# Seven-product weight sums by accumulating transfers from GpSimd, with the products rearranged so that every weight sum is an addition

## The chip, the cores and the metric

One core of one Trainium2 chip runs the whole program. The metric is the device time of one execution in microseconds (us), the median of several runs; smaller is better.

## What is computed

The reference is two layers of a decoder trunk for one sequence of 256 tokens with 1024 channels. A layer is a SwiGLU block (`ffn1`), a token mixer (a diagonal state-space group beside a gated group), and a second SwiGLU block (`ffn2`), each behind an RMSNorm and added to the residual stream:

```
for l in range(2):
    x = x + 0.5 * swiglu(rmsnorm(x, norm_ffn1[l]), ffn1_w_in[l], ffn1_w_out[l])
    x = x + mixer(rmsnorm(x, norm_mix[l]))
    x = x + 0.5 * swiglu(rmsnorm(x, norm_ffn2[l]), ffn2_w_in[l], ffn2_w_out[l])
swiglu(h, w_in, w_out): g, u = split(h @ w_in); return (silu(g) * u) @ w_out     # 1024 -> 2 x 2816 -> 1024
```

All data are float32. The change lies in the last product of `ffn2`, `(silu(g) * u) @ ffn2_w_out`, with 2816 rows of weights.

## The kernel before

**Precision and the weight stream.** Each matmul operand is split into a high part (`w_hi`, rounded to the fp32r type by ScalarE) and a remainder (`w_lo`, by VectorE), and a product is three matmuls: high by high, high by low, low by high. SyncE loads the weights in slots of 1 MB (`raw`, three of them); a slot is two "halves" of 128x1024 weights, and the stream has 152 halves for each layer. ScalarE makes `w_hi` of a half (L1016), VectorE its `w_lo` (L1324). Both have a ring of four halves, so ScalarE starts the split of half n when TensorE is done with half n-4. SyncE loads into a slot when VectorE has split what lay there.

**The order of the work.** Every engine has one written-out order. In `ffn2` ScalarE and VectorE run a loop over h (halves 0 to 43 are the input weights, 44 to 65 the output weights): gates (`gate`, L1070) and hidden tiles at given h, then the split of half h, then at given h the work on the weight sums.

**Seven products.** For six pairs of 128-row tiles of `ffn2_w_out` (SEVEN, L72) the 2x2 blocks are multiplied with seven products in place of eight (Winograd's form). With B11, B12 the two column halves of the first row tile and B21, B22 of the second, it needs four sums of weights T1 to T4 (and four of hidden blocks, S1 to S4). Such a pair is called sum m here, m = 0 to 5 within a layer. Its steps:

- SyncE loads both row tiles into an area of four 128x512 quarters, in two transfers of 512 KB (`load_sums`, L375 to L390), at h = 26, 28, 36, 38, 52, 54 of its own, earlier order (LOAD_AT, L76). Areas 0 and 1 (`sums_b`) serve sums 0 to 3, two further ones (`area`) sums 4 and 5.
- VectorE forms T1 to T4 in place with four subtractions (`sums_make`, L1327 to L1340), at h = 25, 29, 36, 41, 53, 56 (SUMS_AT, L77). T2 needs T1, and T4 needs T2.
- ScalarE splits the 128x2048 area into `s_hi` (`sums_split`, L986 to L994) and VectorE into `s_lo` (L1342 to L1348), at h = 28, 31, 55, 57, 59, 61 (SPLIT_AT, L78). `s_hi` and `s_lo` have two buffers. On ScalarE the step stands behind the split of half h and ahead of the split of half h+1, in one queue.
- TensorE does the seven products (`seven_rows`, L729): three with the plain weights, then four that wait for `s_lo`.

GpSimd prepares the mixer's tables, does the mixer's small operations (`mix`, L1840 to L1876) and the reciprocal square roots of the norms (`norm`, L1667). It issues no transfers. In `ffn2` it waits for the next norm.

Of the kernel before, what the change touches and what calls it, by code (L numbers as in the profile page):

```python
# [11 lines left out]
ALU = mybir.AluOpType  # L12
# [7 lines left out]
UB = FF // 256  # L20
# [53 lines left out]

AREA = (0, 1, 0, 1, 2, 3)
LOAD_AT = (26, 28, 36, 38, 4 * UB + 8, 4 * UB + 10)  # L76
SUMS_AT = (25, 29, 36, 41, 4 * UB + 9, 4 * UB + 12)  # L77
SPLIT_AT = (28, 31, 4 * UB + 11, 4 * UB + 13, 4 * UB + 15, 4 * UB + 17)  # L78
FOLD_AT = 4 * UB + 2 * SEVEN[-1] + 5

S3, S1, S2, S4 = range(4)
T3, T1, T2, T4 = range(4)

B11, B22, B21 = range(3)

# [28 lines left out]
def norm_no(l, i):  # L114
    return 3 * l + i
# [23 lines left out]
def build(nc, a, out):  # L139
    stack = ExitStack()  # L140
    with stack:
# [169 lines left out]
        def hidden_bank(l, j, b):  # L311

            c0, _, t0, t1_ = ROLES[l, stage_of(2 * j)]
            if b == UB - 1:
                return bank[2 * c0]
            return bank[2 * (t1_ if b in (2, 3, 6, 7) else t0) + b % 2]
# [15 lines left out]
        def _(sp):  # L332
# [42 lines left out]
            def load_sums(l, h):  # L375

                for i in range(N7):
                    if LOAD_AT[i] == h:
                        m = l * N7 + i
                        if i == 0:  # L380
                            sp.wait_ge(half_done, half(l, UP2) + 1)
                        if i in (2, 3):
                            sp.wait_ge(slo_done, m - 1)
                        if i > 3:
                            sp.wait_ge(half_done, half(l, DN2))
                        k = 2 * SEVEN[i]
                        src = a["ffn2_w_out"][l, k * P:(k + 2) * P, :].rearrange("(t p) m -> p t m", p=P)
                        dst = areas[AREA[i]].rearrange("p (t c m) -> p t c m", t=2, c=2)
                        for c in range(2):
                            sp.dma_start(dst[:, :, 1 - c, :], src[:, :, c * 512:c * 512 + 512]).then_inc(s_full[AREA[i]], 16)  # L390

            def load_ffn(l, j):
                w_in, w_out = (a["ffn1_w_in"], a["ffn2_w_in"])[j], (a["ffn1_w_out"], a["ffn2_w_out"])[j]
# [589 lines left out]
        def _(act):  # L983
            A = nc.scalar.activation

            def sums_split(l, h):  # L986

                for i in range(N7):
                    if SPLIT_AT[i] == h:
                        m = l * N7 + i  # L990
                        act.wait_ge(sb_done, 4 * m + 4)
                        if m > 1:
                            act.wait_ge(seven_done, m - 1)
                        A(s_hi[:, m % 2, :], areas[AREA[i]], ACT.Copy).then_inc(shi_done, 1)  # L994
# [87 lines left out]
            def hidden_hi(l, j, b):  # L1082
                act.wait_ge(hT_done, UB * (2 * l + j) + b + 1)
                if j and b in SEVEN:
                    m = l * N7 + SEVEN.index(b)
                    act.wait_ge(sa_done, 3 * m)
                    A(a21[:, 0, :], hidden_bank(l, j, b)[:, P:2 * P], ACT.Copy)
                    A(a21[:, 1, :], hidden_bank(l, j, b)[:, P:2 * P], ACT.Copy, scale=-1.0).then_inc(a21_done, 1)
                A(h_hi[:, 2 * b:2 * b + 2, :].rearrange("p k c -> p (k c)"), hidden_bank(l, j, b)[:, :],
                  ACT.Copy).then_inc(hhi_done, 1)  # L1090

# [214 lines left out]
        def _(dve):  # L1306
# [17 lines left out]
                TT(w_lo[:, n % RING, :], raw[:, s, (n % 2) * 1024:(n % 2) * 1024 + 1024],  # L1324
                   w_hi[:, n % RING, :].bitcast(F32), ALU.subtract).then_inc(lo_done, 1)

            def sums_make(l, h):  # L1327

                for i in range(N7):
                    if SUMS_AT[i] == h:  # L1330
                        m = l * N7 + i
                        q = areas[AREA[i]].rearrange("p (i m) -> p i m", i=4)
                        dve.wait_ge(*sums_full(m))
                        TT(q[:, T1, :], q[:, 0, :], q[:, T1, :], ALU.subtract).then_inc(sb_done, 1)
                        dve.wait_ge(sb_done, 4 * m + 1)
                        TT(q[:, T3, :], q[:, 0, :], q[:, 2, :], ALU.subtract).then_inc(sb_done, 1)
                        dve.wait_ge(sb_done, 4 * m + 2)
                        TT(q[:, T2, :], q[:, 2, :], q[:, T1, :], ALU.subtract).then_inc(sb_done, 1)
                        dve.wait_ge(sb_done, 4 * m + 3)
                        TT(q[:, T4, :], q[:, 3, :], q[:, T2, :], ALU.subtract).then_inc(sb_done, 1)  # L1340

            def sums_split(l, h):  # L1342

                for i in range(N7):
# [86 lines left out]
            def hidden_lo(l, j, b):  # L1431
                if j and b in SEVEN:
                    m = l * N7 + SEVEN.index(b)
                    tiles = hidden_bank(l, j, b)[:, :].rearrange("p (i m) -> p i m", i=4)
                    dve.wait_ge(a21_done, m + 1)
                    if m > 0:
                        dve.wait_ge(salo_done, m)
                    dve.wait_ge(hhi_done, UB * (2 * l + j) + b + 1)
                    TT(sums_a[:, 0:2, :], tiles[:, 0:4:3, :], a21[:, :, :], ALU.subtract).then_inc(sa_done, 1)
                    dve.wait_ge(sa_done, 3 * m + 1)  # L1440
                    TT(sums_a[:, S2, :], sums_a[:, S1, :], tiles[:, 0, :], ALU.subtract).then_inc(sa_done, 1)
                    dve.wait_ge(sa_done, 3 * m + 2)
                    TT(sums_a[:, S4, :], tiles[:, 2, :], sums_a[:, S2, :], ALU.subtract).then_inc(sa_done, 1)
                dve.wait_ge(hhi_done, UB * (2 * l + j) + b + 1)
                TT(h_lo[:, 2 * b:2 * b + 2, :].rearrange("p k c -> p (k c)"), hidden_bank(l, j, b)[:, :],  # L1445
                   h_hi[:, 2 * b:2 * b + 2, :].rearrange("p k c -> p (k c)").bitcast(F32),
                   ALU.subtract).then_inc(hlo_done, 1)
# [7 lines left out]
            def fold(l, j):  # L1455


                c0, c1, t0, t1_ = ROLES[l, "ffn2"]
                p5, p6, p7 = bank[2 * c0 + 1], bank[2 * t0], bank[2 * t0 + 1]
                p1, u2, u3 = (sums_b[:, 0, i * 512:i * 512 + 512] for i in range(3))  # L1460
                xb = [[x[:, t, c * 512:c * 512 + 512] for c in range(2)] for t in range(2)]
                n = 8 * l
                dve.wait_ge(p1_done, l + 1)
                STT(u2, p6[:, :], 0.5, p1, ALU.mult, ALU.add).then_inc(fold_done, 1)
                STT(xb[0][1], p5[:, :], 0.5, xb[0][1], ALU.mult, ALU.add).then_inc(fold_done, 1)
                STT(xb[1][1], p5[:, :], 0.5, xb[1][1], ALU.mult, ALU.add).then_inc(fold_done, 1)
                TT(xb[0][0], xb[0][0], p1, ALU.add).then_inc(fold_done, 1)
                dve.wait_ge(fold_done, n + 4)
                STT(u3, p7[:, :], -0.5, u2, ALU.mult, ALU.add).then_inc(fold_done, 1)
                TT(xb[0][1], xb[0][1], u2, ALU.add).then_inc(fold_done, 1)  # L1470
                dve.wait_ge(fold_done, n + 5)
                TT(xb[1][0], xb[1][0], u3, ALU.add).then_inc(fold_done, 1)
                TT(xb[1][1], xb[1][1], u3, ALU.add).then_inc(fold_done, 1)

            def ffn(l, j):
                f = 2 * l + j
                if f == 0:
                    first_in()
                elif j == 0:
                    norm_in(l, 0, UPS[j], ACC_FFN2, (0.5, 0.5), DN2 + FT - 1)  # L1480
                else:
                    norm_in(l, 2, UPS[j], ACC_SSM, (ors[:, 2:3], ors[:, 3:4]), OUT + KT - 1)
                for h in range(4 if f else 5, 4 * UB + FT + 1):
                    if h in GATES_AT[f]:
                        hidden(l, j, GATES_AT[f][h])
                    split(l, UPS[j] + h)
                    if j:
                        sums_split(l, h)
                        sums_make(l, h)
                    if j and h - 1 in HIDDEN_AT and HIDDEN_AT.index(h - 1) in SEVEN:  # L1490
                        sums_lo(l, HIDDEN_AT.index(h - 1))
                    if h in HIDDEN_AT:
                        hidden_lo(l, j, HIDDEN_AT.index(h))
                    if j and h == FOLD_AT:
                        fold(l, j)
# [146 lines left out]
        def _(pool):  # L1642
# [197 lines left out]
            def mix(l):  # L1840
# [34 lines left out]
                inv_sqrt(ors[:, 2:4], oms[:, 2:4], ors_done)  # L1875
                norm(norm_no(l, 2))  # L1876

            link(nc.gpsimd.memset(ident[:, :], 0.0))
            link(nc.gpsimd.affine_select(out=ident[:, :], in_=ident[:, :], compare_op=ALU.not_equal, fill=1.0,
                                         base=0, pattern=[[-1, P]], channel_multiplier=1))  # L1880
# [14 lines left out]
            prep_rest(0)  # L1895
            restart()
            mix(0)
            norm(norm_no(1, 0))
            pool.wait_ge(half_done, half(1, 0))
            clear_blocks()  # L1900
# [1 line left out]
            prep_rest(1)  # L1902
            restart()
            mix(1)
            pool.wait_ge(ms_done, 3 * DEPTH + 1)
            inv_sqrt(rstd_c[:, 0:1], ms_c[:, 0:1], rstd_done)
            pool.wait_ge(x_done, residuals(DEPTH - 1, ACC_FFN2) + 3)
# [22 lines left out]
```

## Time and profile before

| | us |
|---|---|
| median of 3 runs (908.05 to 908.76) | 908.31 |
| the profiled execution, time | 907.8 |
| the profiled execution, span on the core | 906.1 |

The profile is of one execution. Its span leaves out 1.7 us that lie around it. The views used below are the page (busy time by engine, DMA issues), the waits (who waited for whom, longest first), the timeline (instructions in order of time), the windows (busy time and DMA share in given stretches) and the instructions of one tile. PE is TensorE, PEld its weight loads, ACT ScalarE, DVE VectorE, POOL GpSimd, SP SyncE; "SPq" is what SyncE's queue issued. TensorE's granted clock is 0.999 over the span. Layer 0's `ffn2` runs from about 270 to 453 us, layer 1's from about 717 to 900 us.

### The profile page before, as it was taken

How to read it: one execution, taken by the hardware profiler on the slowest of the kernel's cores; microseconds unless marked ns; L12 is line 12 of the kernel's file. 1: busy time of each engine (PE TensorE's matmuls, PEld its weight loads, DVE VectorE, ACT ScalarE, POOL GpSimd, SP SyncE). 2: the span in 40 equal slices, each digit the busy share in tenths (PEclk: the TensorE clock that was granted, in tenths of full speed). 3: DMA queues.
4: the chain of work that ended last, by engine and by line, in shares of the span. 5: the costliest groups of instructions: out<-in, count | busy, mean ns of one | idle time of the engine just before them, and what ended most of it. 6: DMA issues, size and time to landing. Idle time of an engine off the chain costs nothing.

```text
span 906.1 us, 12882 instructions
## 1 busy us (share of the span) xinstructions
PE 897.4 (99%) x4935; PEld 743.1 (82%) x4935; DVE 620.3 (68%) x729; ACT 507.4 (56%) x741; POOL 371.8 (41%) x574
## 2 busy tenths in 40 slices
PE   9999999999999999999999999999999999999997
PEld 7888888888878888887888888888888888888886
DVE  5555665458976578868965656653888855789597
ACT  6544454458766456646464445445677654656474
POOL 3488999894510000000055889988734100000000
PEclk9999999999999999999999999999999999999999
DMA  9786555544256677684559665555344476785751
GB/s 281 196 271 188 186 184 180 175 160 142 94 194 200 196 251 230 229 283 159 186 175 246 186 188 186 186 186 186 120 160 143 139 221 196 263 270 188 267 175 46
DMA packets 138381, 174.60 MB, mean 193 GB/s; under 512 B 18760, under 2 KB 110032, under 8 KB 138320
## 3 DMA queue, kind: packets, MB, share of 16 engines
q1 hardware_dynamic: 138032, 173.24, 59.7%
q8 instruction: 39, 0.64, 0.3%
q10 hardware_dynamic: 288, 0.53, 0.2%
q14 instruction: 22, 0.18, 0.1%
HBM read 172.70 MB, written 1.05 MB: 192 GB/s over the span
## 4 chain that ended last, share of the span: by engine, by line
PE 95%; DVE 3%; issue 1%; DMA 1%; ACT 1%; SPq 0%; ACTq 0%; DVEq 0%
PE bank L501 29%; PE bank L503 29%; PE bank L502 29%; PE bank L606 2%; DVE w_lo L1319 1%; PE bank L511 1%; PE bank L833 1%; DVE s_lo L1348 1%; DMA raw<-in_ffn_w_in 1%; PE bank L861 0%; PE bank L851 0%; PE bank L874 0%; PE bank L716 0%; ACT w_hi L1007 0%; PE bank L937 0%
## 5 line engine op out<-in xcount | busy, mean ns | idle before, releaser
L1324 DVE TENSOR_TENSOR w_lo<-raw,w_hi 128x1024 fp32r<-128x1024 f32 x278 | 351.0, 1271 | 214.4 <-ACT w_hi L1016 214.2
L1016 ACT ACTIVATE w_hi<-raw 128x1024 fp32r<-128x1024 f32 x278 | 292.7, 1061 | 242.0 <-PE bank L503 223.2
L501 PE MATMUL bank<-w_hi,x_hi 128*128 128x512 f32 x856 | 336.5, 393 | 0.0
L503 PE MATMUL bank<-w_hi,x_lo 128*128 128x512 f32 x856 | 333.5, 390 | 0.0
L502 PE MATMUL bank<-w_lo,x_hi 128*128 128x512 f32 x856 | 333.2, 389 | 0.0
L501 PEld LDWEIGHTS bank<-w_hi,x_hi 128*128 128x128 f32 x856 | 160.7, 188 | 35.2 <-issue 2.5
L503 PEld LDWEIGHTS bank<-w_hi,x_lo 128*128 128x128 f32 x856 | 160.7, 188 | 33.7
L502 PEld LDWEIGHTS bank<-w_lo,x_hi 128*128 128x128 f32 x856 | 160.8, 188 | 32.3
L1664 POOL TENSOR_TENSOR rstd_c<-ms_c,neg_half 128x2 f32<-128x2 f32 (+1 forms) x7 | 7.7, 1106 | 394.9 <-DVE ms_c L1367 394.9
L501 PE MATMUL bank<-w_hi,h_hi 128*128 128x512 f32 (+1 forms) x283 | 111.0, 392 | 0.0
L503 PE MATMUL bank<-w_hi,h_lo 128*128 128x512 f32 (+1 forms) x283 | 109.7, 387 | 0.0
L502 PE MATMUL bank<-w_lo,h_hi 128*128 128x512 f32 (+1 forms) x283 | 109.6, 387 | 0.0
L1079 ACT ACTIVATE sil<-bank,rstd_c 128x256 f32<-128x256 f32 x88 | 36.8, 470 | 53.2 <-PE bank L503 53.1
L501 PEld LDWEIGHTS bank<-w_hi,h_hi 128*128 128x128 f32 x283 | 53.1, 188 | 11.4 <-DVE h_lo L1445 0.6
L503 PEld LDWEIGHTS bank<-w_hi,h_lo 128*128 128x128 f32 x283 | 53.1, 188 | 11.0
L502 PEld LDWEIGHTS bank<-w_lo,h_hi 128*128 128x128 f32 x283 | 53.2, 188 | 10.4
L1655 POOL TENSOR_TENSOR sc<-sc 128x16 f32<-128x16 f32 (+1 forms) x154 | 55.2, 358 | 12.3
L1428 DVE SCALAR_TENSOR_TENSOR hid<-bank,rstd_c,sil 128x256 f32<-128x256 f32 x88 | 38.5, 479 | 24.4 <-ACT sil L1079 24.4
L1655 POOL TENSOR_TENSOR pt<-sc,bp 128x256 f32<-128x256 f32 x56 | 52.6, 940 | 4.4
L1658 POOL TENSOR_SCALAR sc<-sc 128x16 f32<-128x16 f32 (+1 forms) x90 | 38.7, 430 | 7.7
L1655 POOL TENSOR_TENSOR bp<-pt 128x256 f32<-128x256 f32 x32 | 36.3, 1133 | 2.5
L1319 DVE TENSOR_TENSOR w_lo<-raw,w_hi 128x1536 fp32r<-128x1536 f32 x12 | 21.0, 1753 | 12.9 <-ACT w_hi L1007 12.9
(231 smaller groups left out, 886.9 us busy)
## 6 DMA issues: line engine op xcount, KB each, us to landing
raw<-in_ffn_w_in SPq DMA_DIRECT2D x172, 512.0 KB
raw<-in_ffn_w_out SPq DMA_DIRECT2D x32, 1024.0 KB
raw<-in_mix_w_in SPq DMA_DIRECT2D x12, 1024.0 KB
raw<-in_mix_w_out SPq DMA_DIRECT2D x8, 1024.0 KB
sums_b<-in_ffn_w_out SPq DMA_DIRECT2D x16, 512.0 KB, 6.9
raw<-in_ffn_w_out SPq DMA_DIRECT2D x12, 512.0 KB
area<-in_ffn_w_out SPq DMA_DIRECT2D x8, 512.0 KB, 6.4
raw<-in_ffn_w_out SPq DMA_DIRECT2D x12, 256.0 KB
```

Of the source, the lines that this page charges most:

```text
L501: mm(o, hi_a, hi_b, start=first, stop=False)
L502: mm(o, hi_a, lo_b, start=False, stop=False)
L503: return mm(o, lo_a, hi_b, start=False, stop=last)
L511: ins = nc.tensor.transpose(turned(pair, j)[:, h * P:h * P + P], x[:, h, k * P:k * P + P], ident[:, :])
L606: ins = nc.tensor.transpose(hidden_bank(l, j, b)[:, c:c + P], hid[:, b % 4, h, ft * P:ft * P + P], ident[:, :])
L1016: A(w_hi[:, n % RING, :], raw[:, s, (n % 2) * 1024:(n % 2) * 1024 + 1024], ACT.Copy).then_inc(hi_done, 1)
L1079: A(sil[:, b % 2, t, :], bank[2 * pair + t][:, 0:256], ACT.Silu, scale=rstd_c[:, t:t + 1]).then_inc(sil_done, 1)
L1319: TT(w_lo[:, n % RING:n % RING + 2, :].rearrange("p s m -> p (s m)")[:, 0:1536], raw[:, s, 0:1536], w_hi[:, n % RING:n % RING + 2, :].rear ...
L1324: TT(w_lo[:, n % RING, :], raw[:, s, (n % 2) * 1024:(n % 2) * 1024 + 1024], w_hi[:, n % RING, :].bitcast(F32), ALU.subtract).then_inc(lo_d ...
L1428: STT(hid[:, b % 4, t, :], bank[2 * pair + t][:, 256:512], rstd_c[:, t:t + 1], sil[:, b % 2, t, :], ALU.mult, ALU.mult).then_inc(hid_done, 1)
L1655: link(nc.gpsimd.tensor_tensor(o, x0, x1, op))
L1658: link(nc.gpsimd.tensor_scalar(o, x0, s1, s2, op0, op1))
```

## The change

The four sums of a pair are formed without VectorE. SyncE loads B12 into two quarters (a source that is repeated), and B21, B22 into the other two. GpSimd then issues four transfers that add to their destination in SBUF: T1 = B12 + B11 and T3 = B12 + B22 from HBM; when both have landed, T2 = B22 + T1, and when that has landed, T4 = B21 + T2, both from SBUF to SBUF. It waits for the last of each sum before the next sum. All six sums of a layer stand in GpSimd's order between `mix` and the next layer's first norm. ScalarE's split waits for the semaphore that these transfers raise. The signs move to the hidden sums (`a21`, `sums_a`), where two copies of ScalarE become one, and to the fold at the stage's end.

```diff
-SUMS_AT = (25, 29, 36, 41, 4 * UB + 9, 4 * UB + 12)
...
-T3, T1, T2, T4 = range(4)
+T1, T3, T4, T2 = range(4)
...
# load_sums (SyncE)
-                        dst = areas[AREA[i]].rearrange("p (t c m) -> p t c m", t=2, c=2)
-                        for c in range(2):
-                            sp.dma_start(dst[:, :, 1 - c, :], src[:, :, c * 512:c * 512 + 512]).then_inc(s_full[AREA[i]], 16)
+                        dst = areas[AREA[i]].rearrange("p (t m) -> p t m", t=2)
+                        b12 = src[:, 0, 512:1024].unsqueeze(1).broadcast_to([P, 2, 512])
+                        sp.dma_start(dst[:, 0, :].rearrange("p (c m) -> p c m", c=2), b12).then_inc(s_full[AREA[i]], 16)
+                        sp.dma_start(dst[:, 1, :], src[:, 1, :]).then_inc(s_full[AREA[i]], 16)
...
# sums_split (ScalarE)
-                        act.wait_ge(sb_done, 4 * m + 4)
+                        act.wait_ge(sb_done, 64 * m + 64)
...
# hidden_hi (ScalarE)
-                    A(a21[:, 0, :], hidden_bank(l, j, b)[:, P:2 * P], ACT.Copy)
-                    A(a21[:, 1, :], hidden_bank(l, j, b)[:, P:2 * P], ACT.Copy, scale=-1.0).then_inc(a21_done, 1)
+                    A(a21[:, :, :], hidden_bank(l, j, b)[:, :].rearrange("p (i m) -> p i m", i=4)[:, 1:4:2, :],
+                      ACT.Copy).then_inc(a21_done, 1)
...
# sums_make leaves VectorE (four subtractions for each sum)
-                        TT(q[:, T1, :], q[:, 0, :], q[:, T1, :], ALU.subtract).then_inc(sb_done, 1)
...
# hidden_lo (VectorE)
-                    TT(sums_a[:, 0:2, :], tiles[:, 0:4:3, :], a21[:, :, :], ALU.subtract).then_inc(sa_done, 1)
+                    TT(sums_a[:, 0:2, :], tiles[:, 0:2, :], a21[:, :, :], ALU.subtract).then_inc(sa_done, 1)
...
-                    TT(sums_a[:, S4, :], tiles[:, 2, :], sums_a[:, S2, :], ALU.subtract).then_inc(sa_done, 1)
+                    TT(sums_a[:, S4, :], tiles[:, 2, :], sums_a[:, S2, :], ALU.add).then_inc(sa_done, 1)
...
# fold (VectorE): the same eight operations, three of them with another sign
...
# new on GpSimd, called as sums_make(0) behind mix(0) and sums_make(1) behind mix(1)
+            def sums_make(l):
+                for i in range(N7):
+                    m = l * N7 + i
+                    k = 2 * SEVEN[i]
+                    b1, b2 = (a["ffn2_w_out"][l, (k + t) * P:(k + t + 1) * P, :] for t in range(2))
+                    q = areas[AREA[i]].rearrange("p (i m) -> p i m", i=4)
+                    pool.wait_ge(*sums_full(m))
+                    pool.dma_start(q[:, T1, :], b1[:, 0:512], accum_op=ALU.add).then_inc(sb_done, 16)
+                    pool.dma_start(q[:, T3, :], b2[:, 512:1024], accum_op=ALU.add).then_inc(sb_done, 16)
+                    pool.wait_ge(sb_done, 64 * m + 32)
+                    pool.dma_start(q[:, T2, :], q[:, T1, :], accum_op=ALU.add).then_inc(sb_done, 16)
+                    pool.wait_ge(sb_done, 64 * m + 48)
+                    pool.dma_start(q[:, T4, :], q[:, T2, :], accum_op=ALU.add).then_inc(sb_done, 16)
+                    pool.wait_ge(sb_done, 64 * m + 64)
```

## Rows read from the trace of the kernel before

**Rows 1.** The page, busy time of each engine, its share and instructions.

```profile
PE 897.4 (99%) x4935; PEld 743.1 (82%) x4935; DVE 620.3 (68%) x729; ACT 507.4 (56%) x741; POOL 371.8 (41%) x574
```

**Rows 2.** The waits, whole run: who waited for whom; total us, times, longest us.

```profile
POOL rstd_c L1664 <- DVE ms_c L1367: 394.9, 7, 182.5
ACT w_hi L1016 <- PE bank L503: 223.2, 153, 3.0
...
PEld bank L501 <- DVE s_lo L1348: 1.5, 2, 0.7
```

**Rows 3.** Timeline, 424 to 432 us: start, duration, engine, line, operation, [idle before].

```profile
425.23 0.68 DVE L1334 TENSOR_TENSOR area<-area 128x512 f32<-128x512 f32 x1
...
428.01 2.28 DVE L1348 TENSOR_TENSOR s_lo<-sums_b,s_hi 128x2048 fp32r<-128x2048 f32 x1
...
429.64 0.39 PE L503 MATMUL bank<-w_hi,h_lo 128*128 128x512 f32 x1
...
430.34 0.19 PEld L501 LDWEIGHTS bank<-s_hi,hs_hi 128*128 128x128 f32 x1 [0.74 <-DVE s_lo L1348]
```

**Rows 4.** Instructions of the tile sums_b: duration in ns, minimum/median/maximum, first and last start.

```profile
L1334 DVE TENSOR_TENSOR sums_b<-sums_b x8: 684/684/685, 336.5 to 831.3; 128x512 f32<-128x512 f32 x8
...
L994 ACT ACTIVATE s_hi<-sums_b x8: 1900/1918/1930, 343.4 to 869.6; 128x2048 fp32r<-128x2048 f32 x8
```

**Rows 5.** Timeline of SyncE's queue, 318 to 370 and 764 to 830 us.

```profile
324.89 1.02 SPq L390 DMA_DIRECT2D sums_b<-in_ffn_w_out  x2
...
332.82 1.02 SPq L390 DMA_DIRECT2D sums_b<-in_ffn_w_out  x2
336.63 18.93 SPq L345 DMA_DIRECT2D raw<-in_ffn_w_in  x8
...
771.76 1.02 SPq L390 DMA_DIRECT2D sums_b<-in_ffn_w_out  x2
```

**Rows 6.** DMA issues between 325.2 and 326.0 us: KB each, median us to landing.

```profile
sums_b<-in_ffn_w_out SPq DMA_DIRECT2D x2, 512.0 KB, 6.3
```

**Rows 7.** Timeline of ScalarE, 322 to 376 and 785 to 810 us.

```profile
343.42 1.90 ACT L994 ACTIVATE s_hi<-sums_b 128x2048 fp32r<-128x2048 f32 x1
...
350.55 0.84 ACT L1079 ACTIVATE sil<-bank,rstd_c 128x256 f32<-128x256 f32 x2 [1.60 <-PE bank L503]
...
352.23 1.92 ACT L994 ACTIVATE s_hi<-sums_b 128x2048 fp32r<-128x2048 f32 x1
...
361.43 0.84 ACT L1079 ACTIVATE sil<-bank,rstd_c 128x256 f32<-128x256 f32 x2 [1.60 <-PE bank L503]
...
807.73 0.84 ACT L1079 ACTIVATE sil<-bank,rstd_c 128x256 f32<-128x256 f32 x2 [1.60 <-PE bank L503]
```

**Rows 8.** Timeline of VectorE, 322 to 352 us.

```profile
345.35 2.29 DVE L1348 TENSOR_TENSOR s_lo<-sums_b,s_hi 128x2048 fp32r<-128x2048 f32 x1 [0.58 <-ACT s_hi L994]
347.56 1.22 DVE L1324 TENSOR_TENSOR w_lo<-raw,w_hi 128x1024 fp32r<-128x1024 f32 x1
```

**Rows 9.** Windows, all engines: busy us by engine (count), PEclk, DMA share, GB/s.

```profile
332.00:340.00 8.00, 8.00 (x37) 6.63 (x36) 7.60 (x13) 4.42 (x8) 0.00 (x0) 1.00 0.85 291
340.00:348.00 8.00, 8.00 (x37) 6.64 (x36) 6.91 (x7) 5.38 (x7) 0.00 (x0) 1.00 0.73 235
348.00:356.00 8.00, 8.00 (x37) 6.62 (x36) 7.90 (x10) 5.50 (x7) 0.00 (x0) 1.00 0.45 137
```

**Rows 10.** DMA issues of the run: count, KB each, median us from issue to landing.

```profile
raw<-in_ffn_w_in SPq DMA_DIRECT2D x8, 256.0 KB, 4.7
...
out<-x SPq DMA_DIRECT2D x6, 128.0 KB, 2.1
```

**Rows 11.** The tile sums_b: landing times of its sixteen loads.

```profile
DMA to landing us min/median/max: 6.0/6.9/8.6
```

**Rows 12.** The page, costliest groups: the only GpSimd group on the norms.

```profile
L1664 POOL TENSOR_TENSOR rstd_c<-ms_c,neg_half 128x2 f32<-128x2 f32 (+1 forms) x7 | 7.7, 1106 | 394.9 <-DVE ms_c L1367 394.9
```

**Rows 13.** Timeline of TensorE, 439 to 441 us.

```profile
440.00 0.39 PE L501 MATMUL bank<-s_hi,hs_hi_last 128*128 128x512 f32 x1
```

More of the change, by code:

```diff
@@ L1325, in split @@
                    w_hi[:, n % RING, :].bitcast(F32), ALU.subtract).then_inc(lo_done, 1)
[L1327 to L1333, printed above, removed]
-                        TT(q[:, T1, :], q[:, 0, :], q[:, T1, :], ALU.subtract).then_inc(sb_done, 1)
[L1335 to L1340, printed above, removed]
             def sums_split(l, h):
@@ L1468, in fold @@
                 dve.wait_ge(fold_done, n + 4)
-                STT(u3, p7[:, :], -0.5, u2, ALU.mult, ALU.add).then_inc(fold_done, 1)
-                TT(xb[0][1], xb[0][1], u2, ALU.add).then_inc(fold_done, 1)
+                STT(u3, p7[:, :], 0.5, u2, ALU.mult, ALU.add).then_inc(fold_done, 1)
+                TT(xb[0][1], xb[0][1], u2, ALU.subtract).then_inc(fold_done, 1)
                 dve.wait_ge(fold_done, n + 5)
                 TT(xb[1][0], xb[1][0], u3, ALU.add).then_inc(fold_done, 1)
-                TT(xb[1][1], xb[1][1], u3, ALU.add).then_inc(fold_done, 1)
+                TT(xb[1][1], xb[1][1], u3, ALU.subtract).then_inc(fold_done, 1)
             def ffn(l, j):
@@ L1488, in ffn @@
                         sums_split(l, h)
-                        sums_make(l, h)
                     if j and h - 1 in HIDDEN_AT and HIDDEN_AT.index(h - 1) in SEVEN:
@@ L1897, in _ @@
             mix(0)
+            sums_make(0)
             norm(norm_no(1, 0))
@@ L1904, in _ @@
             mix(1)
+            sums_make(1)
             pool.wait_ge(ms_done, 3 * DEPTH + 1)
```

## The prediction, made before the changed kernel was run

> **What bounds the kernel now.** I read the busy times first: TensorE works 897.4 of the 906.1 us of the span, 99% [rows 1]. So the kernel can only become faster where TensorE stands still, and slower wherever something new makes it stand still. The waits come next. ScalarE waits for TensorE 153 times in the weight splits alone, 223.2 us in all, while the waits of TensorE's weight loads for VectorE's `s_lo` are two, one in each layer [rows 2]. The engines that prepare weights are ahead of TensorE and are paced by its ring of four halves. VectorE's 620.3 us are therefore mostly cover, not path.
>
> The one place where the sums on VectorE hurt is seen in the timeline. From 425.23 us VectorE makes the last pair's four sums, and only at 428.01 does it start an `s_lo` whose `s_hi` was ready before; TensorE's last matmul starts at 429.64, the next weight load at 430.34 [rows 3]. At the pace of 0.23 us between matmuls (2.72 us for twelve, below) it should have come at 429.87, so about 0.5 us are lost, and 0.1 us more as the first matmul starts cold. That is 0.6 us, in each layer.
>
> **What the change removes.** Twelve sums of four subtractions leave VectorE: 48 x 0.69 us = 33 us [rows 4], which is 5% of its busy time. All but the sums of rows 3 lie in time that VectorE has. With them gone, the `s_lo` of rows 3 starts some 2.7 us earlier, and both stalls go: **-1.2 us** for the two layers. That is the whole gain that I can find. Twelve copies of ScalarE, the other signs in the fold and in the hidden sums, and the new quarters cost or give nothing: the copies lie beside ScalarE's 223 us of waiting [rows 2], the rest are the same operations on the same shapes. SyncE still issues two transfers of 512 KB for a sum.
>
> **What it adds.** GpSimd gets 48 transfers of 256 KB and waits for them. Behind them in its queue stands only the next layer's norm; GpSimd waits 394.9 us for VectorE's means anyway [rows 2], so the wait costs there nothing. What waits for the transfers is ScalarE: the split of the area stands in its queue ahead of the next weight split. So the question is when the chain of a sum ends: landing, then the pair T1 and T3, then T2, then T4, three steps in series, and the second sum's chain only behind the first's.
>
> *When they may end.* Sum 0 is split at 343.42, sum 1 at 352.23 [rows 7], but later would do. The gates wait for halves 27 and 31; they start at 350.55 and 361.43 [rows 7], so a half takes 10.88/4 = 2.72 us, half 29 begins at 353.3 and half 32 at 361.4. Behind a late sum 1 stand ScalarE's `s_hi` (1.92 us [rows 4]), VectorE's `s_lo` (2.29) and `w_lo` of half 32 (1.22) [rows 8], and some 0.2 us of signals: 5.6 us. So sum 1 must be ready at 361.4 - 5.6 = **355.8**, and sum 0 in the same way at 347.7. In layer 1 the way from the first load's issue (771.76) to the same gate (807.73) is 36.0 us against 36.5 in layer 0 [rows 5, 7]: 0.6 us less room.
>
> *When they can begin.* Sum 0's second load is issued at about 325.4 [rows 5] and lands 6.3 us later [rows 6], at 331.7. Sum 1's loads, issued from 332.82, land by 340, before sum 0's chain is through. So both chains together may take 355.8 - 331.7 = **24.1 us**.
>
> *What a chain takes.* No row shows a transfer from GpSimd or one that adds. From below: a quiet 128 KB store takes 2.1 us from issue to landing [rows 10]. The queue moves 291 GB/s at a share of 0.85 [rows 9], 342 GB/s when full, so its 128 KB are 0.38 us of that and 256 KB are 0.77. A step is then at least 2.5 us, the pair 3.3, a chain 8.3, two chains 16.6: no stall. From above: every step like the slowest load of 8.6 us [rows 11], 25.8 us for a chain. Between them I build a step from three terms. The fixed part is 2.1 - 0.38 - 0.5 (SyncE's own issue, half of 1.02 [rows 5]) = 1.2 us. The issue by GpSimd I take as its small operation, 1.1 us [rows 12], as its instructions cost more than SyncE's. The data take 0.77 us once, or 1.54 if the destination's reading counts like a second transfer; where SyncE's queue is full they take twice as long, since the two share the same 16 engines. It is nearly full from 332 to 343 (share 0.85, then 0.73, with the weights issued at 336.63 [rows 5]), and far less from 348 (0.45 [rows 9]).
>
> - Data once: sum 0 is pair 5.4 + T2 3.8 + T4 3.1 = 12.3 us; sum 1, in the quiet part, 3.8 + 3.1 + 3.1 = 10.0. Both 22.3: in time.
> - Data twice: 8.5 + 5.4 + 3.8 = 17.7 and 5.4 + 3.8 + 3.8 = 13.0. Both 30.7: sum 1 is ready at 362.4, 6.6 us late, and 7.2 us late in layer 1.
>
> I take the middle, 26.5 us, which makes a busy step 4.6 us, close to the 4.7 us of SyncE's 256 KB loads at the kernel's busy start [rows 10]. Sum 1 is then ready at 358.2: 2.4 us late, 3.0 us in layer 1. TensorE stands still for that time, as its ring of halves has run dry; nothing later gives it back, as TensorE is busy for 99% of the span [rows 1]. The other four sums have room: at 13.3 us a chain the sixth would end at 331.7 + 80 = 412, and TensorE wants it at 440.00 [rows 13], less 4.4 us for its splits.
>
> Weights delayed by the sharing cost nothing: those issued at 336.63 are split from about 347.9 on, and the extra 1 MB (2 if counted twice) of sum 0 is 3 to 6 us of the queue's time; were the cover gone, it would be 1 to 2 us a layer.
>
> **The sum.** -1.2 + 2.4 + 3.0 = +4.2 us on the profiled execution's 907.8 us, 912.0. That execution is 0.5 us below the median of 908.3, so I predict **912.5 us**.
>
> **The rivals.**
> *In time.* Both chains fit into 24.1 us, ScalarE never waits, and only the gain is left: 908.3 - 1.2 = 907.1 us, not slower. For it speaks the bound from below, and the sum with data counted once; against it the full queue at the very time of sum 0 [rows 9]. It decides at 12 us a chain. The Trainium skill (DMA: Bandwidth & Descriptors, Anatomy of one DMA) gives a transfer issued by GpSimd 2.0 us plus its bytes at 436 GB/s, all told: by that, as an estimate, 2.6 us a step, 0.6 more for the pair, 8.4 us a chain and 907.1 us. The page's fit is for plain copies; no run so far shows one here.
> *Six in series.* If adding is much slower than copying, the six chains of a layer follow each other past the stage's end: the sixth must be ready at 440.0 - 4.4 = 435.6, so from (435.6 - 331.7)/6 = 17.3 us a chain it rules. At 20 us it ends 16.1 us late in each layer, +31 us, 939 us; at the upper bound of 25.8 us, 50.9 late, +101, 1009 us. Against it: it needs steps like the slowest loads, also in the quiet parts.
> *VectorE's relief pays more.* 33 us are taken off VectorE, but the waits of TensorE's weight loads for `s_lo` add up to 1.5 us [rows 2]; over 1.8 us could only come from something that no wait shows.
>
> **How the numbers follow.** What a measurement of this kernel can tell from no change is about 0.2%, 1.8 us. The stall of sum 1 has 0.50, with its own range from 909 to 925 us (data twice gives 921.5, and a slower issue lies above). In time has 0.35, six in series 0.11, more relief 0.04. Faster by over 0.2% is the last alone, 0.04. Within 0.2% is the rival in time and the edge of the stall where it eats the gain, 0.36. Slower is the rest, 0.60. The range goes from 906.8, just under the rival in time, to 936, which leaves out most of six in series.
>
> **What the changed profile would show.** The wait of ScalarE's L994 for GpSimd's transfers, long for sum 1 of each layer, near 352 and 798 us of the old time, and behind it waits of TensorE for `w_lo` of a few us: the forecast. No such wait, and landing times of 2 to 3.5 us: the rival in time. L994 waiting at the sixth sum: six in series. The stall behind rows 3 should be gone in any case. I am wrong if TensorE stands still elsewhere, above all for weights from SyncE, or if GpSimd's issue or the adding takes times outside my bounds.

## The result, and the profile after

The changed kernel takes 972.4 us (median of five runs, 968.3 to 974.3) against 908.1 us: a ratio of 1.0694, 95% interval 1.0677 to 1.0711, or 64 us more. The prediction was slower, 912.5 us, with a range up to 936. The direction was right, the size was not: it lies in the span that the rival *six in series* was given, 939 to 1009 us.

The page of the profile after (span 972.5 us), busy times, answers to [rows 1]:

```profile
span 972.5 us, 12882 instructions
...
PE 912.2 (94%) x4935; PEld 752.4 (77%) x4935; DVE 589.8 (61%) x681; ACT 505.4 (52%) x729; POOL 415.1 (43%) x622
```

TensorE has the same 4935 matmuls. It stands still for 972.5 - 912.2 = 60.3 us, against 8.7 us before: +51.6. And it is busy 14.8 us longer. Together that is the 66.4 us by which the spans differ. VectorE lost 30.5 us of work, and nothing came of it.

The waits of the profile after (total us, times, longest us) tell for what:

```profile
ACT s_hi L994 <- DMA sums_b<-sums_b: 50.5, 4, 14.3
...
PE bank L501 <- DVE w_lo L1324: 32.1, 4, 9.7
...
ACT s_hi L994 <- DMA area<-area: 28.0, 3, 13.5
...
PE bank L501 <- DVE s_lo L1333: 19.6, 2, 9.9
```

GpSimd waits for each landing before it issues the next step. ScalarE's `s_hi` waits for the last landing, and behind it stands the weight split. TensorE then waits for `w_lo`, four times in all, two in each layer; and for the `s_lo` of the sixth sum, once in each. 32.1 + 19.6 = 51.7 us are the whole +51.6.

The timeline of GpSimd in layer 0 shows the chains of sums 0 and 1, L1870 being T1, L1873 T2 and L1875 T4, with L1871 (T3) directly behind each L1870 (start, duration, then in brackets the wait before):

```profile
334.03 1.10 POOL L1870 DMA_DIRECT2D sums_b<-in_ffn_w_out  x1 [54.58 <-DMA sums_b<-in_ffn_w_out]
...
345.65 0.88 POOL L1873 DMA_DIRECT2D sums_b<-sums_b  x1 [9.59 <-DMA sums_b<-in_ffn_w_out]
352.41 0.90 POOL L1875 DMA_DIRECT2D sums_b<-sums_b  x1 [5.89 <-DMA sums_b<-sums_b]
355.99 0.89 POOL L1870 DMA_DIRECT2D sums_b<-in_ffn_w_out  x1 [2.67 <-DMA sums_b<-sums_b]
...
362.44 0.87 POOL L1873 DMA_DIRECT2D sums_b<-sums_b  x1 [4.66 <-DMA sums_b<-in_ffn_w_out]
368.08 0.90 POOL L1875 DMA_DIRECT2D sums_b<-sums_b  x1 [4.76 <-DMA sums_b<-sums_b]
375.52 0.89 POOL L1870 DMA_DIRECT2D sums_b<-in_ffn_w_out  x1 [6.54 <-DMA sums_b<-sums_b]
```

Sum 0 takes 21.7 us from its first issue to ScalarE's start (355.73 below), sum 1 a further 19.5. ScalarE's timeline, the three splits that waited:

```profile
355.73 1.91 ACT L994 ACTIVATE s_hi<-sums_b 128x2048 fp32r<-128x2048 f32 x1 [11.23 <-DMA sums_b<-sums_b]
...
375.26 1.91 ACT L994 ACTIVATE s_hi<-sums_b 128x2048 fp32r<-128x2048 f32 x1 [14.06 <-DMA sums_b<-sums_b]
...
466.69 1.91 ACT L994 ACTIVATE s_hi<-area 128x2048 fp32r<-128x2048 f32 x1 [13.55 <-DMA area<-area]
```

They answer to 343.42 and 352.23 in [rows 7] and to the sixth sum, for which the prediction worked out 435.6 from [rows 13].

The early stops also hold back what comes later. SyncE issues the load of sum 4, the fifth of the layer, 21.5 us later than before the change, and GpSimd waits for it before it can begin that chain (first line from the kernel before, the other two from the changed kernel):

```profile
395.86 0.88 SPq L390 DMA_DIRECT2D area<-in_ffn_w_out  x2
...
417.36 0.37 SPq L389 DMA_DIRECT2D area<-in_ffn_w_out  x1
...
425.38 0.88 POOL L1870 DMA_DIRECT2D area<-in_ffn_w_out  x1 [10.93 <-DMA area<-in_ffn_w_out]
```

The windows of layer 0 (busy us of PE, PEld, DVE, ACT, POOL with counts, granted clock, DMA share, GB/s) show what a stop does to TensorE's clock:

```profile
335.00:345.00 10.00, 10.00 (x46) 8.27 (x45) 6.92 (x11) 5.49 (x7) 1.06 (x2) 1.00 1.04 296
...
355.00:365.00 10.00, 3.85 (x11) 3.06 (x12) 6.48 (x6) 5.47 (x6) 2.67 (x3) 0.66 0.61 133
365.00:375.00 10.00, 6.04 (x27) 4.67 (x25) 0.00 (x0) 0.00 (x0) 0.90 (x1) 0.97 1.01 291
375.00:385.00 10.00, 4.22 (x11) 3.35 (x12) 7.62 (x7) 6.42 (x7) 2.60 (x3) 0.51 0.49 90
```

In the stretches where TensorE starts again after a stop the mean granted clock is 0.66 and 0.51; the timeline has the matmuls at 363 us 0.43 us apart, from 364.3 on 0.23. So TensorE restarts at the lower level, 1.2 GHz, and the timeline shows the same slower pace behind all six stops, which are 6.6 to 9.9 us long. Against 0.23 us a matmul the matmuls behind the stops lose 13.9 us, 1.5 to 2.9 us a stop, which is nearly all of the 14.8 us of longer busy time. GpSimd's queue and its transfers in the DMA view (packets, MB and share of the 16 engines' span; KB each, median us from issue to landing):

```profile
q0 software_dynamic: 6912, 12.59, 7.6%
...
sums_b<-in_ffn_w_out POOLq DMA_DIRECT2D x16, 256.0 KB, 5.9
sums_b<-sums_b POOLq DMA_DIRECT2D x16, 256.0 KB, 6.3
...
area<-in_ffn_w_out POOLq DMA_DIRECT2D x8, 256.0 KB, 7.0
area<-area POOLq DMA_DIRECT2D x8, 256.0 KB, 4.3
```

### The profile page after: what moved, and what is told of

It is laid out like the page before. It is cut to its first block, busy times and chain, and to the rows that moved or that the text cites. A ratio compares the mean times of both kernels' runs of the same rounds, so it can differ in the third digit from the quotient of the medians.

```text
span 972.5 us, 12882 instructions
## 1 busy us (share of the span) xinstructions
PE 912.2 (94%) x4935; PEld 752.4 (77%) x4935; DVE 589.8 (61%) x681; ACT 505.4 (52%) x729; POOL 415.1 (43%) x622
## 3 DMA queue, kind: packets, MB, share of 16 engines
q0 software_dynamic: 6912, 12.59, 7.6%
## 4 chain that ended last, share of the span: by engine, by line
PE 75%; DMA 16%; issue 4%; DVE 2%; ACT 1%; SPq 1%; POOL 1%; POOLq 0%; ACTq 0%
PE bank L501 23%; PE bank L502 23%; PE bank L503 23%; DMA sums_b<-in_ffn_w_out 5%; DMA area<-in_ffn_w_out 4%; DMA sums_b<-sums_b 3%; DMA area<-area 3%; PE bank L606 1%; DVE s_lo L1333 1%; PE bank L511 1%; PE bank L833 1%; ACT s_hi L994 1%; DMA x<-in_x 1%; DVE w_lo L1324 0%; PE bank L861 0%
## 5 line engine op out<-in xcount | busy, mean ns | idle before, releaser
L501 PE MATMUL bank<-w_hi,x_hi 128*128 128x512 f32 x856 | 340.9, 398 | 32.1 <-DVE w_lo L1324 32.1
L502 PE MATMUL bank<-w_lo,x_hi 128*128 128x512 f32 x856 | 336.6, 393 | 0.0
L501 PEld LDWEIGHTS bank<-w_hi,x_hi 128*128 128x128 f32 x856 | 163.0, 190 | 69.8 <-issue 21.9
L503 PEld LDWEIGHTS bank<-w_hi,x_lo 128*128 128x128 f32 x856 | 162.7, 190 | 34.7
L502 PEld LDWEIGHTS bank<-w_lo,x_hi 128*128 128x128 f32 x856 | 163.1, 191 | 32.9
L1870 POOL DMA_DIRECT2D sums_b<-in_ffn_w_out x8 | 7.4, 920 | 140.8 <-DMA sums_b<-in_ffn_w_out 109.7
L1639 POOL TENSOR_TENSOR sc<-sc 128x16 f32<-128x16 f32 (+1 forms) x154 | 59.6, 387 | 12.3
L502 PEld LDWEIGHTS bank<-w_lo,h_hi 128*128 128x128 f32 x283 | 53.3, 188 | 10.4
L1333 DVE TENSOR_TENSOR s_lo<-sums_b,s_hi 128x2048 fp32r<-128x2048 f32 x8 | 18.3, 2293 | 54.0 <-ACT s_hi L994 54.0
L994 ACT ACTIVATE s_hi<-sums_b 128x2048 fp32r<-128x2048 f32 x8 | 15.3, 1914 | 55.3 <-DMA sums_b<-sums_b 50.5
```

What stands on the lines that cost most here:

```text
L501: mm(o, hi_a, hi_b, start=first, stop=False)
L502: mm(o, hi_a, lo_b, start=False, stop=False)
L503: return mm(o, lo_a, hi_b, start=False, stop=last)
L1333: TT(s_lo[:, m % 2, :], areas[AREA[i]], s_hi[:, m % 2, :].bitcast(F32), ALU.subtract).then_inc(slo_done, 1)
L1639: link(nc.gpsimd.tensor_tensor(o, x0, x1, op))
```

## The experiments

The comparison for each is the kernel before on the same chip. "Changed" means that the edit is made in the changed kernel.

**The form alone (e1).** The kernel before with the four subtractions of `sums_make` as additions and the signs moved as in the change.

```diff
-TT(q[:, T1, :], q[:, 0, :], q[:, T1, :], ALU.subtract)
+TT(q[:, T1, :], q[:, 0, :], q[:, T1, :], ALU.add)
```

> The new form of the products alone: the four weight sums of a pair are additions, the signs are moved to the hidden sums and the fold, but VectorE still forms the weight sums and SyncE loads as before. If the time of the changed kernel comes from the waits for GpSimd's transfers, this one stands at 908 us, within 1 us of the kernel before. If the new form itself costs (another order of signs, one copy of ScalarE in place of two), it stands above 910 us.

908.07 us, ratio 1.0001 (0.9992 to 1.0009). The form costs nothing; the 64 us belong to the transfers, SyncE's new loads or the waits for them.

**The transfers with nobody waiting (e2).** e1, and on GpSimd, after `mix`:

```diff
+pool.wait_ge(*sums_full(m))
+pool.dma_start(q[:, 0, :], b1[:, 0:512], accum_op=ALU.add).then_inc(pad_done, 16)     # q: two quarters of a spare area
...
+pool.wait_ge(pad_done, 64 * m + 64)
```

> As e1, and beside it GpSimd issues the same 48 adding transfers, triggered by the same landings and chained in the same way, but into a spare area that nobody reads (its sums are no part of the output). If the serial waits are the cause, the transfers cost TensorE nothing: 908 us, within 2 us. If the cause is that they share the DMA engines with SyncE's weights, much of the 64 us shows here as well: 925 us or more, with TensorE's stops traced back to raw loads.

915.14 us, ratio 1.0083 (1.0068 to 1.0098): above the 908 that I expected and below the 925 of the rival. TensorE's waits hold no raw load. Most of the rest is at the end of the kernel:

```profile
ACT x L1287 <- POOL rstd_c L1666: 6.3, 1, 6.3
```

The last norm stands in GpSimd's queue behind the sixth chain, which nothing held back here, and ScalarE waited 6.3 us for it (0.9 us in e10 below). That is 5.4 of the 6.9 us by which the span grew; another 1.6 us is a wait of TensorE for the input `x` at 15 us, long before GpSimd's first transfer. So sharing the DMA engines costs TensorE nothing that shows; a late chain costs wherever something is queued behind it, on GpSimd too.

**Copies in place of adding transfers (e3).** Changed, with `accum_op` left out in all four lines; the additions of the weight sums are left out with it.

> The changed kernel with GpSimd's transfers as plain copies: the additions of the weight sums are left out, so the sums hold wrong values, but every issue, wait and chain stays. If a step is long because the transfer stands behind SyncE's queued loads, only the second reading of the data goes, 0.7 us of a step's 6: three serial steps for each of six sums, at most 13 us a layer, so 945 to 965 us. If it is the adding that makes a step long, the chains fall under 12 us and the time under 920 us.

923.09 us, ratio 1.0166 (1.0152 to 1.0180): between the two, near the rival's side. TensorE's stops shrink to this:

```profile
PE bank L501 <- DVE w_lo L1324: 12.4, 4, 4.7
...
q0 software_dynamic: 3840, 12.59, 3.8%
```

Only sums 0 and 1 are late, and the sixth is in time. The same 12.59 MB take 3.8% of the DMA engines' time in place of 7.6%: adding takes the engines twice the time of copying. Sum 0's chain fell from 21.7 to 17.6 us (first issue at 333.00, ScalarE's start at 350.56), sum 1's from 19.5 to 12.3. Sums 4 and 5 take 14.7 and 18.0 us from 409.45 on, where sum 4's load has landed, in place of 19.9 and 21.4. I had counted the saving for one step and not asked what it does at the thresholds: the sixth sum is on time, and its stop goes altogether.

**Early loads (e5), interleaved chains (e6), both (e7).** Changed, with

```diff
-LOAD_AT = (26, 28, 36, 38, 4 * UB + 8, 4 * UB + 10)
+LOAD_AT = (10, 14, 36, 38, 4 * UB + 8, 4 * UB + 10)     # e5, e7
...
-for i in range(N7):                                     # e6, e7: two sums at a time, T1 and T3 of both,
+for i in range(0, N7, 2):                               # then T2 of both, then T4 of both; sb_two[0], sb_two[1]
```

> The changed kernel with the loads of sums 0 and 1 at h = 10 and 14 in place of 26 and 28, some 45 us sooner, when their areas are already free. If the time is set by where each chain ends against where ScalarE's order wants it, the stops at sums 0 and 1 vanish and the sixth sum alone is late, as chains of 21 us from about 402 us on end 10 us late: 925 to 940 us, with one stop of TensorE in each layer. If the long time comes from anything else, for instance the sharing of the DMA engines during the whole stage, it stays above 955 us.

> The changed kernel with GpSimd's chains of sums 0 and 1, 2 and 3, 4 and 5 interleaved: it issues the first pair of transfers of both before it waits, then T2 of both, then T4 of both, with a semaphore for each. The transfers are the same. If a chain is long because landings follow each other, the second sum of a pair is ready some 5 us behind the first in place of 20: the stop at sum 0 stays, those at sums 1 and 5 go, 920 to 940 us. If the DMA engines are short of throughput, the two chains slow each other and it stays above 955 us.

> Early loads of sums 0 and 1 and interleaved chains together. If the ends of the chains against ScalarE's order are all that matters, sums 4 and 5, whose loads land at about 402 and 406 us, are ready by about 430, just when they are wanted, and the kernel is back at 907 to 912 us. If it stays above 920 us, something else than late chains costs time.

e5: 940.33 us, ratio 1.0361 (1.0345 to 1.0377). e6: 931.49, ratio 1.0258 (1.0244 to 1.0272). e7: 907.02, ratio 0.9991 (0.9982 to 1.0000). The same 48 transfers cost 64 us or nothing, by where their chains end. In e5 the sixth sum of layer 0 is split at 446.12, 10.5 us after the 435.6 that I had worked out, and TensorE's stop there is 10.4 us. I had expected one stop in each layer; in layer 1 there are two, as sum 4 is late too (3.2 and 7.9 us), and the time lies at the upper end of what I gave. In e7 TensorE's matmuls have no wait for `w_lo` or `s_lo` in their list, and ScalarE's for the sums are short:

```profile
ACT s_hi L995 <- DMA area<-area: 8.6, 6, 1.9
...
PE bank L967 <- POOLq L1886: 1.7, 1, 1.7
```

e7 also bounds what the freed VectorE is worth: its median is 0.9 us below, with an interval from nothing to 1.6 us, which holds the 1.2 us of the prediction.

**The load of sum 1 later (e8).** Changed, `LOAD_AT[1]` 30 in place of 28.

> The changed kernel with SyncE's load of sum 1 at h = 30 in place of 28, so that its 1 MB is not queued just ahead of sum 0's first pair of transfers (which landed 9 to 11 us after its issue). If a transfer of GpSimd stands behind what SyncE issued before it, that first pair lands about 3 us sooner, within 6 to 7 us. If the two queues share the engines evenly, it changes by less than 1.5 us. The time of the whole kernel is no test here, as the load of sum 1 then falls on the next steps: 965 to 975 us.

967.55 us, ratio 1.0656 (1.0636 to 1.0675). The first pair is issued at 333.44 and T2, which waits for it, at 341.62:

```profile
333.44 1.11 POOL L1870 DMA_DIRECT2D sums_b<-in_ffn_w_out  x1 [54.06 <-DMA sums_b<-in_ffn_w_out]
...
341.62 0.88 POOL L1873 DMA_DIRECT2D sums_b<-sums_b  x1 [6.14 <-DMA sums_b<-in_ffn_w_out]
```

That is 8.2 us, against 11.6 in the changed kernel: 3.4 us less (in layer 1 7.6 against 10.9), about the time of the 1 MB (3.1 us at 342 GB/s) that is no longer issued just around it. This alone does not tell standing behind that load from sharing with it: the bound of 1.5 us that I gave for an even sharing was too low, as the pair itself needs 3.3 us of all the engines (below), and two such loads that share evenly delay each other by about 3 us. The DMA view tells more (packets, MB, share of the 16 engines). The changed kernel from 334 to 338 us, and from 338 to 344:

```profile
q1 hardware_dynamic: 1106, 1.16, 97.4%
...
q1 hardware_dynamic: 536, 1.11, 56.4%
q0 software_dynamic: 280, 0.52, 47.6%
```

e8 from 334 to 337 us, and from 337 to 340:

```profile
q1 hardware_dynamic: 840, 0.84, 95.4%
...
q0 software_dynamic: 222, 0.42, 83.0%
q1 hardware_dynamic: 194, 0.18, 18.2%
```

q0 is GpSimd's queue, q1 SyncE's. In both kernels no packet of the pair moves for 3 to 4 us, while the 1 MB of weights passes that SyncE issued at 332.8. Some 1.3 us of that is the transfer's own lead: in layer 1 of the changed kernel a T4 issued at 943.19, with both queues empty, moves its first packet after 944.5. After that the pair shares the engines about evenly with the load of sum 1 in the changed kernel, and has them nearly to itself in e8. Most of the 3.4 us is this sharing; the standing behind earlier loads is there in both.

**Half the room for descriptors (e9).** Changed, `dynamic_dma_scratch_size` 512 in place of 1024.

> The changed kernel with 512 bytes in place of 1024 per partition for the descriptors of GpSimd's transfers, nothing else. In the changed kernel GpSimd's second transfer of sums 2 and 5 of each layer is issued 3.5 to 6.3 us late with no wait that the profile names (issue), four times, always twelve transfers apart by the half. If that is a lack of room for descriptors until earlier transfers are done, half the room makes such waits about twice as many, and the chains of more sums longer: 975 to 1000 us. If it is something else, four such waits stay, at 966 to 974 us.

984.95 us, ratio 1.0845 (1.0813 to 1.0876). In the changed kernel the second transfer of sums 2 and 5 is issued late, four times in the two layers. Now it is in every sum, twelve times:

```profile
POOL sums_b L1871 <- issue: 38.3, 8, 8.1
POOL area L1871 <- issue: 28.3, 4, 7.8
```

So these waits go with the room for descriptors: half the room made three times as many, where I had expected twice. More room was not tried.

**What makes a landing long (e10, e11, e12).** e2 with the transfers on the spare area as copies; as adding transfers of half the columns; of half the rows.

```diff
-pool.dma_start(q[:, 0, :], b1[:, 0:512], accum_op=ALU.add)
+pool.dma_start(q[:, 0, :], b1[:, 0:512])                                   # e10
+pool.dma_start(q[:, 0, 0:256], b1[:, 0:256], accum_op=ALU.add)             # e11
+pool.dma_start(q[0:64, 0, :], b1[0:64, 0:512], accum_op=ALU.add)           # e12
```

> As e2, with the 48 transfers on the spare area as plain copies, so that both run beside the same steady stream of weights and nothing of TensorE's stops comes back on them. In e2 they landed 7.0 us (from HBM) and 5.7 us (SBUF to SBUF) after issue. If a transfer only moves its bytes at half the rate when it adds, copies land 0.7 us sooner: 5 us or more. If a transfer's time grows with the number of its packets, each of which waits behind a stretch of SyncE's, copies (80 packets each in e3, against 144 when adding) land in little more than half the time over the quiet 3 us: 4 to 5 us. The kernel takes 908 to 912 us.

> As e2 with adding transfers of 256 columns in place of 512: half the bytes in the same 128 rows, so as many packets of half the size (half of each sum is left out on the spare area). By bytes a landing falls by 0.7 us where it is quiet and by 1 to 2 us under load. By packets it stays where it was under load, 6 to 7 us from HBM and 5 to 6 us between quarters.

> As e2 with adding transfers of 64 of the 128 rows: half the bytes and half the packets of full size (the other rows are left out on the spare area). By packets landings fall to 4 to 5 us under load, as for copies, and half the descriptors leave fewer late issues. By bytes they fall no more than with half the columns.

All three take the time of before: 908.35 us (0.9992 to 1.0015), 908.16 (0.9988 to 1.0010), 908.12 (0.9989 to 1.0012). Their DMA issues, of e2 first, then e10, e11, e12 (KB each, median us to landing):

```profile
pad<-in_ffn_w_out POOLq DMA_DIRECT2D x24, 256.0 KB, 7.0
pad<-pad POOLq DMA_DIRECT2D x24, 256.0 KB, 5.7
```

```profile
pad<-in_ffn_w_out POOLq DMA_DIRECT2D x24, 256.0 KB, 5.3
pad<-pad POOLq DMA_DIRECT2D x24, 256.0 KB, 4.6
```

```profile
pad<-in_ffn_w_out POOLq DMA_DIRECT2D x24, 128.0 KB, 5.3
pad<-pad POOLq DMA_DIRECT2D x24, 128.0 KB, 5.0
```

```profile
pad<-in_ffn_w_out POOLq DMA_DIRECT2D x24, 128.0 KB, 6.5
pad<-pad POOLq DMA_DIRECT2D x24, 128.0 KB, 5.1
```

The theory of packets (each of a transfer's packets waits behind a stretch of SyncE's) falls: by it e12, with 3840 packets like e10, should land like e10, and e11, with 6912 like e2, like e2. It is the other way round: e11 lands sooner than e12. Copying in place of adding saves 1.1 to 1.7 us, half the bytes 0.5 to 1.7. But all of them stay at 4.6 us or more, where the shortest landing was 2.3 us for a copy (e10) and 3.3 for an adding transfer (e2). So most of what load adds does not go with the transfer's own size. The transfers fall at somewhat different times in these four kernels, so differences of some tenths of a us say little.

**One step later on VectorE (e4).** The kernel before, the last pair's sums on VectorE one step later.

```diff
-SUMS_AT = (25, 29, 36, 41, 4 * UB + 9, 4 * UB + 12)
+SUMS_AT = (25, 29, 36, 41, 4 * UB + 9, 4 * UB + 13)
```

> The kernel before with one number changed: VectorE forms the last pair's sums one step later in its order, behind the s_lo that TensorE waited for. If the gain that the prediction found is real (0.6 us in each layer from that one wait), this takes 907 us, 0.13% less than before. If that wait only gives way to another, it takes 908 us or more.

906.95 us, ratio 0.9988 (0.9979 to 0.9997). The wait for `s_lo` of [rows 2] is gone from its list. The median is 0.9 us below the kernel before, and the interval just leaves out no change. One number gives as much as the freed VectorE gave in e7.

## Why the prediction was right in direction and wrong in size

**What held.** The direction was no luck: the path is the forecast one, a late chain, ScalarE's split behind it, TensorE waiting for `w_lo`. TensorE loses only where it is made to stand still, and VectorE's 33 us were cover: e7 without them gains 0.9 us at the median, little clear of noise. The gain of 1.2 us fits e4 and e7, which both lie 0.9 us below the kernel before. The deadlines held: in layer 0 sum 0 was split 8.0 us after its 347.7 and TensorE's two stops for `w_lo` add up to 16.7 us, where sum 1's 375.26 - 355.8 = 19.5 us was the bound; in e5 the sixth sum's 10.5 us gave a stop of 10.4. The weights from SyncE were not delayed to TensorE's cost (e2, e10 to e12).

**The step that failed** is the term for the data under load in *What a chain takes*. The prediction let a busy queue double a transfer's own time, 0.77 us once or twice to 1.5 or 3.1, and it counted only sum 0's pair and T2 as busy. Its upper bound, "data twice", was 8.5 + 5.4 + 3.8 = 17.7 us for sum 0 and 5.4 + 3.8 + 3.8 = 13.0 for sum 1. By the timeline above, layer 0 took 11.6 + 6.8 + 3.3 = 21.7 and 6.5 + 5.6 + 7.2 = 19.3 us. The terms without load were about right: an adding step alone took 3.3 us, GpSimd's issue was taken as 1.1 us and is 0.87 to 1.25, and the data count twice, as the DMA engines' time shows (7.6% against 3.8% in e3). What was wrong is what load adds. A transfer did not run at half speed from its issue; it stood still until loads that SyncE had issued before it had passed. For sum 0's pair this is seen in e8. For sum 1 the changed kernel shows its pair alone, from 356 to 362 us, and then its T4, which was issued at 368.08, from 368.1 to 372 and from 372 to 375:

```profile
q0 software_dynamic: 288, 0.52, 55.6%
...
q1 hardware_dynamic: 1007, 1.29, 106.6%
...
q0 software_dynamic: 144, 0.26, 48.1%
q1 hardware_dynamic: 146, 0.48, 40.9%
```

The pair alone takes 55.6% of 6 us, 3.3 us of all the engines, close to the 3.1 of the bound. T4 moves nothing for nearly 4 us while SyncE's loads, the last issued at 366.69, pass. It is not VectorE that holds GpSimd up there: the windows above have VectorE idle from 365 to 375 us. So sum 1 did not run in a quiet part. The prediction had read the share up to 356 us (0.45 from 348 [rows 9]); the kernel before has its queue full again behind that, as its DMA view from 356 to 375 us shows:

```profile
q1 hardware_dynamic: 5183, 6.17, 96.7%
```

The Trainium skill (DMA: Bandwidth & Descriptors, Anatomy of one DMA) has 2.0 us plus the bytes at 436 GB/s, 2.6 us for 256 KB as an estimate; the shortest copy of e10, 2.3 us, lies 0.3 us below that, the loaded medians of 4.6 and 5.3 us lie far above it.

**From 13.3 to 20 us a chain.** With that term the first two chains take 21.7 and 19.5 us, and sum 2's, whose second issue waits for room, 24.8. That is over both thresholds of the prediction, 12 us for sum 1 and 17.3 for the sixth. The rival *six in series* had these rows and a price of 31 us at 20 us a chain; it had 0.11, as I held steps like the slowest loads in all parts unlikely. It counted one lateness in each layer, that of the sixth sum against the old time, as if the six chains ran on while TensorE stands still. They do not: sum 4's chain waits for its own load, and the stops at sums 0 and 1 move that load 21.5 us back. So late chains paid three times: 6.9 and 9.7 us at sums 0 and 1, 9.9 us at the sixth in layer 0. It also means that the sixth sum's threshold hangs on two chains and not on six. Sum 4's load lands at about 402.5 us before the change (395.86 and a median of 6.4 us), so (435.6 - 402.5)/2, about 16.5 us a chain, is an estimate of it; that 17.3 lies so near is chance.

**A term that was missing.** After each stop TensorE ran some us at the lower clock level: 14.8 us in all, over a fifth of the loss. The prediction had no term for it beyond 0.1 us for a first matmul.

**A slip.** The bound "data twice" adds up to 908.3 - 1.2 + 6.6 + 7.2 = 920.9 us, not 921.5; nothing hangs on it.

**What stays open.** The traces show GpSimd's transfers standing behind SyncE's earlier loads and sharing with later ones, but not why the engines serve the two queues so. Nor was it told apart how far the burst of SyncE's loads that follows a stop lengthens the chains of sum 1 and later, as the kernel before has a full queue there as well.

## What to carry to other kernels

Moving work from a covered engine to transfers changes no throughput here but puts a latency, in series, ahead of whatever is queued behind the wait: count the landings in the chain, price each by what is measured under the other traffic (here 5.6 to 7.2 us behind SyncE's loads for a step that takes 3.3 alone), and compare the end with the deadline of the queue that waits. If the chain can start earlier or run beside another, do that first: it turned 972 us into 907 with the same transfers. And look for the one wait that the moved work causes; here a change of one step in VectorE's order gave 0.9 us, as much as the move gave at its best.

## What the runs showed of the hardware that was not expected

An adding transfer takes the DMA engines twice the time of a copy of the same bytes (7.6% against 3.8% of the span for 12.59 MB) and 144 packets in place of 80 for 256 KB; its issue takes GpSimd 0.87 to 1.25 us, a copy's mostly 0.55 (e3). With 1024 bytes per partition for descriptors the issue of every twelfth adding transfer waits 3.5 to 6.3 us, with 512 every fourth does, 3.5 to 8.1 us (e9). And a transfer from GpSimd moved no packet for some 3 to 4 us while SyncE's earlier loads passed (97.4% of the engines' time from 334 to 338 us, 106.6% from 368.1 to 372), then shared the engines about evenly with a load that was issued around the same time (47.6% and 56.4% from 338 to 344).
